# Hymba/PEER decoder layer on one core: memory tile transposed over five blocks, convolution halves by ScalarE, one row gather per block

## The chip, the cores and the metric

One core of a Trainium2 chip runs the whole layer. The metric is the device time of one launch in microseconds, as the median of several runs; the profile is of one more launch of the same program.

## The reference, cut to what matters

One decoder layer on 512 tokens of width 1024, all in float32.

```python
h = rmsnorm(x); proj = h @ w_in          # conv B | C | v | hgrn q | f | i | g, 512 columns each
y_conv = rmsnorm(B * conv3(C * v)) ; y_hgrn = hgrn2(q, f, i, g)
x = x + concat(y_conv, y_hgrn) @ w_out
kv = rmsnorm(mem) @ wkv                  # mem: 256 fixed memory tokens
x = x + cross_attention(rmsnorm(x), kv)
h = rmsnorm(x); q = h @ w_query          # 8 heads x 2 x 128
s = q . sub_keys; top-16 of each half -> 256 candidates -> top-16; gate = softmax(best)
# dense form of the expert layer: 128 blocks of 128 experts
hidden = gelu(h @ expert_down.T); y = (gate * hidden) @ expert_up; x = x + y
out = rmsnorm(x)
```

## The kernel before, in words

**Arithmetic.** Each float32 product is made of three matmuls on split operands: high by high, low by high, high by low. A weight block (128 by 1024 values, 512 KB) is loaded by SyncE into a ring of four slots; ACT copies its upper half (`high`, L539, tile `w_high`), POOL subtracts that from the whole (`low`, L432, tile `w_low`), then PE uses the block. A slot is loaded again once PE is done with it, so ACT, POOL and PE move block by block behind each other, at most four blocks apart. Each engine executes its instructions in program order.

**Front part.** Blocks 0 to 11 are column blocks of the input projection. After block 7 PE transposes the normalised memory tile: eight 128 by 128 transposes for chunks 0 to 3 (`turn_tiles`, L1335), then, inside `turn`, two transposes for each of the chunks 4 to 7 (`turn_chunk`, L1321), each of which waits until ACT (`norm_high`, L533) and DVE (`norm_gain`, L900) have taken the chunk four before it out of the same psum bank. Blocks 12 to 15 use psum banks 4 to 7, the banks of the memory tile, behind a wait for all eight chunks. Blocks 28 to 31 and 36 to 39 make the keys of the memory, 32 to 35 its values. Between block 29 and block 30 four matmuls (L1490) sum the squares of the convolution output over channels into psum bank 2; ACT turns that sum into a root (L639, L640); DVE then makes, chunk by chunk, the scaled product (L997), its upper half (L969) and its lower half (L970). The four chunks of the other group have the same two halves and come first. The output product, block 40 on, waits for all eight (`y_ready`).

**Expert part.** The last 128 blocks of the first weight are the down projection. I call them blocks 0 to 127 here; block i of the loops is high/low number 84 + i. For block i ACT makes the upper half of block i + 2, then the GELU of block i (L746), then starts a store of it (L748). The last of the four token tiles is not multiplied densely in full: for one tile (and 16 tokens of another, the "edge") the down rows of the chosen experts are gathered instead, one gather of 128 rows (512 KB) per list slot (`down_row`, L450, on POOL's queue), and DVE takes their dot products (L1069; L1066 for the edge). There are 144 gathers; the first 66 share a ring of seven buffers and stand between POOL's `low` of blocks 0 to 61. Meanwhile DVE chooses the top 16 for three token tiles, one after another (`choose`), with 22 dot products each placed at fixed points in between: numbers 0 to 21, 22 to 43, 44 to 65. Of each tile, `best_ready` comes after the 16th of its dots (number 37 for the second tile, 59 for the third), and the index and gate pieces (`hk_ready`) after the 22nd. ACT waits for `best_ready` of the second tile right before block 32's turn and of the third right before block 52's (the exponential, L778, then goes on with upper halves). PE transposes the pieces (`turn_indices`, L1645) behind block 39, before block 59 and behind block 59. After block 19 ACT starts eight small copies of the edge's row numbers (L783) in a row, and the first edge gather, number 33, waits for them.

**What sets the place of a gather.** In the loop over i, 0 to 61, POOL first executes `low` of block i and then the gathers that a formula gives it:

```python
while k < DOTS_A and i > FIRST_GATHER and (k - RING_A) * (AHEAD - 8 - FIRST_GATHER) < (i - FIRST_GATHER - 1) * (DOTS_A - RING_A):
    down_row(k)
    k += 1
```

With DOTS_A = 66, RING_A = 7 and AHEAD = 60 this is (k - 7) * 52 < (i - 1) * 59, so 59 gathers stand behind 52 blocks, some blocks with two, and the last one (65) stands behind block 53.

## Time and profile before

| what | value |
|---|---|
| median of 3 runs | 1671.52 us (1670.11 to 1676.58) |
| the profiled execution | 1673.48 us |
| its span, first to last instruction | 1671.4 us |
| PE busy | 1634.0 us, 98% |
| DVE busy | 1123.3 us, 67% |
| POOL busy | 891.1 us, 53% |
| ACT busy | 668.0 us, 40% |
| mean granted TensorE clock | 0.996 |

Times of day in the profile are microseconds from the span's start. The profiled execution was 2.0 us above the median. The front part runs to about 520, the choosing and the first 60 down blocks from 540 to 789, the rest of the first product to about 1130, and the second product to the end.

### The profile page before, as it was taken

How to read it: one execution, taken by the hardware profiler on the slowest of the kernel's cores; microseconds unless marked ns; L12 is line 12 of the kernel's file. 1: busy time of each engine (PE TensorE's matmuls, PEld its weight loads, DVE VectorE, ACT ScalarE, POOL GpSimd, SP SyncE). 2: the span in 40 equal slices, each digit the busy share in tenths (PEclk: the TensorE clock that was granted, in tenths of full speed). 3: DMA queues.
4: the chain of work that ended last, by engine and by line, in shares of the span. 5: the costliest groups of instructions: out<-in, count | busy, mean ns of one | idle time of the engine just before them, and what ended most of it. 6: DMA issues, size and time to landing. Idle time of an engine off the chain costs nothing.

```text
span 1671.4 us, 26847 instructions
## 1 busy us (share of the span) xinstructions
PE 1634.0 (98%) x9307; PEld 1452.3 (87%) x9307; DVE 1123.3 (67%) x2165; ACT 668.0 (40%) x980; POOL 891.1 (53%) x501
## 2 busy tenths in 40 slices
PE   8999999999999999999999999999999999999998
PEld 6788788767999999999999999998788878888886
DVE  4154471230283999996988887216878778888888
ACT  5352443341334343534444444433334333333334
POOL 4363374413055888996876666764444444433341
PEclk9999999999999999999999999999999999999999
DMA  5232243213634999997999999949899999999994
GB/s 189 77 101 76 76 139 104 98 39 113 218 114 170 310 330 303 306 322 226 337 337 361 355 358 345 326 166 334 293 345 334 347 317 356 347 338 337 355 341 164
DMA packets 153308, 422.11 MB, mean 253 GB/s; under 512 B 15776, under 2 KB 65952, under 8 KB 153120
## 3 DMA queue, kind: packets, MB, share of 16 engines
q1 hardware_dynamic: 90096, 234.52, 41.0%
q0 software_dynamic: 39168, 142.62, 24.4%
q10 hardware_dynamic: 23984, 44.23, 6.9%
q8 instruction: 30, 0.49, 0.1%
q14 instruction: 30, 0.25, 0.0%
HBM read 376.60 MB, written 44.17 MB: 252 GB/s over the span
## 4 chain that ended last, share of the span: by engine, by line
PE 60%; issue 20%; POOL 13%; DMA 4%; ACT 1%; DVE 1%; ACTq 0%; POOLq 0%; SPq 0%; DVEq 0%
PE psum L1349 19%; PE psum L1351 18%; PE psum L1350 18%; POOL w_low L432 11%; PE psum L1621 4%; POOL arena L450 2%; DMA arena<-up_in 2%; DMA kept<-down_in 1%; DMA arena<-hid_dram 1%; PE psum L1606 1%; ACTq L783 0%; ACT w_high L539 0%; DVE arena L1302 0%; ACT up_high L543 0%; DVE wgt_low L1266 0%
## 5 line engine op out<-in xcount | busy, mean ns | idle before, releaser
L432 POOL TENSOR_TENSOR w_low<-kept,w_high 128x1024 fp32r<-128x1024 f32 x212 | 520.3, 2456 | 405.7 <-ACT w_high L539 404.2
L1349 PE MATMUL psum<-hT_high,w_high 128*128 128x368 f32 (+2 forms) x1408 | 487.9, 347 | 9.9 <-POOL w_low L432 8.1
L1350 PE MATMUL psum<-hT_low,w_high 128*128 128x368 f32 (+2 forms) x1408 | 479.6, 341 | 0.0
L1351 PE MATMUL psum<-hT_high,w_low 128*128 128x368 f32 (+2 forms) x1408 | 479.4, 341 | 0.0
L539 ACT ACTIVATE w_high<-kept 128x1024 fp32r<-128x1024 f32 x212 | 224.1, 1058 | 212.1 <-DMA kept<-down_in 72.8
L1349 PE MATMUL psum<-up_high,wgt_high 128*128 128x512 f32 x768 | 300.1, 391 | 5.5 <-DVE wgt_low L1266 5.5
L1351 PE MATMUL psum<-up_high,wgt_low 128*128 128x512 f32 x768 | 299.4, 390 | 0.0
L1350 PE MATMUL psum<-up_low,wgt_high 128*128 128x512 f32 x768 | 299.4, 390 | 0.0
L1349 PEld LDWEIGHTS psum<-hT_high,w_high 128*128 128x128 f32 x1408 | 264.5, 188 | 25.7 <-POOL w_low L432 13.0
L1351 PEld LDWEIGHTS psum<-hT_high,w_low 128*128 128x128 f32 x1408 | 264.6, 188 | 10.3
L1350 PEld LDWEIGHTS psum<-hT_low,w_high 128*128 128x128 f32 x1408 | 264.8, 188 | 10.0 <-issue 0.5
L543 ACT ACTIVATE up_high<-arena 128x1024 fp32r<-128x1024 f32 x128 | 135.8, 1061 | 320.1 <-DMA arena<-up_in 309.5
L1237 DVE TENSOR_TENSOR up_low<-arena,up_high 128x1024 fp32r<-128x1024 f32 x128 | 156.5, 1222 | 66.1 <-ACT up_high L543 65.2
L490 POOL DMA_INDIRECT kept<-up_in,kept x64 | 101.8, 1591 | 156.2 <-DVE kept L1245 142.7
L490 POOL DMA_INDIRECT arena<-up_in,kept x64 | 108.8, 1700 | 135.4 <-DVE kept L1245 122.6
L1069 DVE CUSTOM_DVE_ANT_0 arena<-arena,psum 128x1024 f32<-128x1024 f32 x128 | 152.8, 1213 | 40.5 <-DMA arena<-down_rows,kept 40.4
L1349 PEld LDWEIGHTS psum<-up_high,wgt_high 128*128 128x128 f32 x768 | 144.5, 188 | 37.8 <-issue 8.1
L1351 PEld LDWEIGHTS psum<-up_high,wgt_low 128*128 128x128 f32 x768 | 144.6, 188 | 30.0
L1350 PEld LDWEIGHTS psum<-up_low,wgt_high 128*128 128x128 f32 x768 | 144.6, 188 | 30.0
L450 POOL DMA_INDIRECT arena<-down_rows,kept x128 | 127.9, 999 | 43.9 <-issue 16.4
L746 ACT ACTIVATE arena<-psum 128x368 f32<-128x368 f32 x112 | 53.5, 477 | 173.7 <-PE psum L1351 172.7
L1214 DVE TENSOR_TENSOR arena<-arena,psum 128x3072 bf16<-128x3072 bf16 x48 | 83.9, 1747 | 0.0
(231 smaller groups left out, 1957.9 us busy)
## 6 DMA issues: line engine op xcount, KB each, us to landing
kept<-down_in SPq DMA_DIRECT2D x128, 512.0 KB, 5.8
arena<-up_in SPq DMA_DIRECT2D x128, 512.0 KB, 5.6
kept<-front_w SPq DMA_DIRECT2D x100, 512.0 KB, 3.3
hid_dram<-arena ACTq DMA_DIRECT2D x112, 184.0 KB, 5.8
arena<-hid_dram SPq DMA_DIRECT2D x112, 184.0 KB, 6.1
gate_dram<-arena ACTq DMA_DIRECT2D x40, 512.0 KB, 7.3
under_w<-gate_dram SPq DMA_DIRECT2D x24, 640.0 KB, 7.3
arena<-gate_dram SPq DMA_DIRECT2D x8, 640.0 KB, 6.9
```

Source lines behind the costliest of these rows:

```text
L432: nc.gpsimd.tensor_tensor(w_low[:, s, :], ring[:, s, :], w_hi[:, s, :].bitcast(F32), ALU.subtract).then_inc(low_ready, 1)
L450: nc.gpsimd.indirect_dma_start(ring[slot], None, down_rows, bass.IndirectOffsetOnAxis((edge_idx if edge else idx3)[:, j:j + 1].bitcast(U32 ...
L490: nc.gpsimd.indirect_dma_start(rows_c[k % RING_C], None, up_rows, bass.IndirectOffsetOnAxis(idx3[:, k:k + 1].bitcast(U32), 0))\
L539: nc.scalar.activation(w_hi[:, s, :], ring[:, s, :], ACT.Copy).then_inc(high_ready, 1)
L543: nc.scalar.activation(up_hi[:, s, :], uraw[:, s, :], ACT.Copy).then_inc(up_high, 1)
L1069: ins = nc.vector.tensor_tensor_reduce(ring[slot], ring[slot], h_row, 1.0, 0.0, ALU.mult, ALU.add, dot3[:, j:j + 1])
L1214: nc.vector.tensor_tensor(hot_g[:, s], hot_i.rearrange("p (n q) i r -> p n q i r", q=1).to_broadcast(each), pieces[:, m:m + PAIRS].rearran ...
L1237: nc.vector.tensor_tensor(up_lo[:, s, :], uraw[:, s, :], up_hi[:, s, :].bitcast(F32), ALU.subtract).then_inc(up_low, 1)
L1349: nc.tensor.matmul(out, lhs[0], rhs[0], start=first, stop=False)
L1350: nc.tensor.matmul(out, lhs[0], rhs[1], start=False, stop=False)
L1351: return nc.tensor.matmul(out, lhs[1], rhs[0], start=False, stop=last)
L1621: ins = nc.tensor.matmul(psum[:, (2 * h + m) % 3, t % 4 * P:(t % 4 + 1) * P], hot_j[:, h % HOTS, t // 2, :, t % 2], hot_g[:, h % HOTS, t / ...
```

## The change

Five edits. The transposes of the memory tile's chunks 4 to 7 go behind blocks 8 to 11, two transposes each, and ACT's and DVE's work on these chunks follows them. ACT copies the upper halves of the four convolution chunks, in between its upper halves of the weights 34 to 37; DVE makes a product, and then the lower half of the chunk before. The sum of squares stands behind block 30. POOL's loop takes one gather per block, from block 1 on. The eight copies of the edge's row numbers stand three behind ACT's work on block 20, three behind 21 and two behind 22.

```diff
-                while k < DOTS_A and i > FIRST_GATHER and (k - RING_A) * (AHEAD - 8 - FIRST_GATHER) < (i - FIRST_GATHER - 1) * (DOTS_A - RING_A):
+                if k < DOTS_A and i > FIRST_GATHER:
                     down_row(k)
                     k += 1
...
                 if b == 7:
-                    norm_high(memn)
+                    norm_high(memn, range(0, 4))
+                if b >= 8:
+                    norm_high(memn, range(b - 4, b - 3))
...
             keys_out(29, 1)
+            keys_out(30, 2)
             act.wait_ge(conv_sum, 1)
...
-            keys_out(30, 2)
             keys_out(31, 3)
             for b in range(32, 36):
                 ahead(b)
+                act.wait_ge(conv_y, CC + b - 31)
+                nc.scalar.activation(hT_half[0][:, b - 32, :], pB[:, b - 32, :], ACT.Copy).then_inc(y_high, 1)
...
             for n in range(DT):
-                early_tiles(TURN_AT[n - 1] if n else 4 + PARTS, EXP_AT[n])
+                for i in range(TURN_AT[0] + 3, TURN_AT[0] + 4) if n == 1 else ():
+                    early_at(i)
+                early_tiles((4 + PARTS, TURN_AT[0] + 4, TURN_AT[1])[n], EXP_AT[n])
...
                     for q in range(PARTS):
+                        if q % 3 == 0:
+                            early_at(TURN_AT[n] + q // 3)
                         act.dma_start(edge_idx[q * EDGE:(q + 1) * EDGE, :],
...
-            for c in range(CC):
-                step(nc.vector.scalar_tensor_tensor(pB[:, c, :], pV[:, c, :], vec[:, V_CONV + c:V_CONV + c + 1],
-                                                    junk[:, SEQ:2 * SEQ], ALU.mult, ALU.mult))
-                y_halves(c, pB[:, c, :])
+            for c in range(CC + 1):
+                if c < CC:
+                    nc.vector.scalar_tensor_tensor(pB[:, c, :], pV[:, c, :], vec[:, V_CONV + c:V_CONV + c + 1],
+                                                   junk[:, SEQ:2 * SEQ], ALU.mult, ALU.mult).then_inc(conv_y, 1)
+                if c:
+                    dve.wait_ge(conv_y, CC + c)
+                    dve.wait_ge(y_high, c)
+                    nc.vector.tensor_tensor(hT_half[1][:, c - 1, :], pB[:, c - 1, :], hT_half[0][:, c - 1, :].bitcast(F32),
+                                            ALU.subtract).then_inc(y_ready, 1)
...
                 columns(b, b % 4, hT_half, SEQ, b % 4)
                 if b == 7:
-                    turn(memn)
+                    turn_tiles(memn)
+                if b >= 8:
+                    pe.wait_ge(memn.ready, b - 7)
+                    turn_chunk(memn, b - 4)
             pe.wait_ge(memn.ready, KC)
...
             keys(29, 1)
+            keys(30, 2)
             pe.wait_ge(conv_sq, CC)
...
-            keys(30, 2)
             keys(31, 3)
```

On POOL, the end of the loop over the blocks 0 to 61 before the change (L432 is `low` of one block, L450 a gather; the last four gathers stand behind the loop):

```order
L450 DMA arena<-down_rows,kept 128x1024 x2
L432 TENSOR_TENSOR w_low<-kept,w_high 128x1024
L450 DMA arena<-down_rows,kept 128x1024
...
L450 DMA arena<-down_rows,kept 128x1024
L432 TENSOR_TENSOR w_low<-kept,w_high 128x1024 x8
L450 DMA arena<-down_rows,kept 128x1024 x4
```

The same place with the change:

```order
L432 TENSOR_TENSOR w_low<-kept,w_high 128x1024
L450 DMA arena<-down_rows,kept 128x1024
L432 TENSOR_TENSOR w_low<-kept,w_high 128x1024
L450 DMA arena<-down_rows,kept 128x1024
L432 TENSOR_TENSOR w_low<-kept,w_high 128x1024 x2
L450 DMA arena<-down_rows,kept 128x1024 x4
```

Gather 65 stood behind `low` of block 53 and now stands behind `low` of block 59; gather 59 stood between the `low` of blocks 47 and 48 and now stands behind 53; gather 33 stood behind 24 and now stands behind 27.

On ACT, the memory tile before (L539 the upper half of a weight block, L569 an output of the input projection, L533 the upper half of a memory chunk), from block 7's output on:

```order
L569 ACTIVATE arena<-psum 128x512
L533 ACTIVATE memT_high<-psum,kept 128x256 x8
L539 ACTIVATE w_high<-kept 128x1024
L569 ACTIVATE arena<-psum 128x512
L539 ACTIVATE w_high<-kept 128x1024
```

and with the change, from the same output to the first of the four later chunks:

```order
L569 ACTIVATE arena<-psum 128x512
L533 ACTIVATE memT_high<-psum,kept 128x256 x4
L539 ACTIVATE w_high<-kept 128x1024
L569 ACTIVATE arena<-psum 128x512
L533 ACTIVATE memT_high<-psum,kept 128x256
```

Four of the eight chunks went behind the outputs of the blocks 8, 9, 10 and 11.

On ACT, from the root of the convolution's sum (its two instructions are the ones that write `kept`) before the change:

```order
L639 ACTIVATE kept<-psum,kept 128x512
L640 ACTIVATE kept<-kept 128x512
L539 ACTIVATE w_high<-kept 128x1024
L627 ACTIVATE arena<-psum 128x256
L539 ACTIVATE w_high<-kept 128x1024
L627 ACTIVATE arena<-psum 128x256
L539 ACTIVATE w_high<-kept 128x1024 x4
L632 ACTIVATE arena<-psum 128x512 x2
```

and with the change:

```order
L642 ACTIVATE kept<-psum,kept 128x512
L643 ACTIVATE kept<-kept 128x512
L539 ACTIVATE w_high<-kept 128x1024
L629 ACTIVATE arena<-psum 128x256
L539 ACTIVATE w_high<-kept 128x1024
L648 ACTIVATE hT_high<-arena 128x512
L539 ACTIVATE w_high<-kept 128x1024
L648 ACTIVATE hT_high<-arena 128x512
...
L634 ACTIVATE arena<-psum 128x512 x2
```

One key block went ahead of the root, and four copies of convolution chunks stand between the upper halves of the weights.

## Rows read from the trace of the kernel before

**Rows 1.** Who waited for whom on PE: us in total, times, longest.

```profile
PE psum L1349 <- POOL w_low L432: 8.1, 10, 2.3
PE psum L1349 <- DVE wgt_low L1266: 5.5, 5, 3.6
PE psum L1349 <- DVE hT_low L970: 2.1, 1, 2.1
```

**Rows 2.** Timeline around the memory tile: start, length, engine, line, idle before.

```profile
60.59 1.03 PE L1335 MATMUL psum<-kept,arena 128*128 128x128 f32 x8
...
63.36 1.56 PE L1321 MATMUL psum<-kept,arena 128*128 128x128 f32 x8 [1.74 <-DVE memT_low L900]
...
71.98 1.06 ACT L539 ACTIVATE w_high<-kept 128x1024 fp32r<-128x1024 f32 x1 [6.54 <-PE psum L1351]
...
77.42 1.06 ACT L539 ACTIVATE w_high<-kept 128x1024 fp32r<-128x1024 f32 x1 [3.90 <-PE psum L1351]
```

**Rows 3.** Timeline in the convolution stretch, PE and DVE.

```profile
205.97 3.70 PE L1490 MATMUL psum<-arena,kept 128*128 128x512 f32 x8 [1.17 <-ACT arena L592]
...
212.36 2.52 DVE L969 CAST hT_high<-arena 128x512 fp32r<-128x512 f32 x1
```

**Rows 4.** Timeline of the down blocks, ACT's queue and PE's gaps.

```profile
623.11 5.39 ACTq L783 DMA_DIRECT2D arena<-arena  x8
...
632.35 0.43 PE L1349 MATMUL psum<-hT_high,w_high 128*128 128x368 f32 x1 [2.29 <-POOL w_low L432]
...
674.01 0.43 PE L1349 MATMUL psum<-hT_high,w_high 128*128 128x368 f32 x1 [1.32 <-POOL w_low L432]
```

**Rows 5.** DMA issues of 560 to 760: count, median us from issue to landing.

```profile
arena<-down_rows,kept POOLq DMA_INDIRECT x39, 6.6
```

**Rows 6.** Timeline, second tile: dot 33, low of block 27, best_ready, exponential.

```profile
647.80 1.23 DVE L1066 CUSTOM_DVE_ANT_1 arena<-arena 128x1024 f32<-128x1024 f32 x1 [1.81 <-DMA arena<-down_rows,arena]
...
649.86 2.42 POOL L432 TENSOR_TENSOR w_low<-kept,w_high 128x1024 fp32r<-128x1024 f32 x1
...
669.30 0.28 DVE L1113 TENSOR_TENSOR arena<-arena 128x128 f32<-128x128 f32 x1
...
673.88 1.28 ACT L778 ACT_TABLE_LOAD   x1 [0.68 <-ACT arena L746]
```

**Rows 7.** Timeline, third tile: dots 55 and 59; low 49, 53, 54; exponential; GELU 53.

```profile
732.15 1.22 DVE L1066 CUSTOM_DVE_ANT_1 arena<-arena 128x1024 f32<-128x1024 f32 x1
...
741.76 2.43 POOL L432 TENSOR_TENSOR w_low<-kept,w_high 128x1024 fp32r<-128x1024 f32 x1
...
749.52 1.20 DVE L1069 CUSTOM_DVE_ANT_0 arena<-arena,psum 128x1024 f32<-128x1024 f32 x1
...
756.09 2.41 POOL L432 TENSOR_TENSOR w_low<-kept,w_high 128x1024 fp32r<-128x1024 f32 x1
...
758.45 1.28 ACT L778 ACT_TABLE_LOAD   x1 [0.68 <-ACT arena L746]
...
761.09 2.42 POOL L432 TENSOR_TENSOR w_low<-kept,w_high 128x1024 fp32r<-128x1024 f32 x1 [1.47 <-ACT w_high L539]
...
765.29 0.48 ACT L746 ACTIVATE arena<-psum 128x368 f32<-128x368 f32 x1 [0.64 <-PE psum L1351]
```

**Rows 8.** Timeline: dot 65, its tile's last piece, low 59, PE's transposes before block 59.

```profile
770.23 1.21 DVE L1069 CUSTOM_DVE_ANT_0 arena<-arena,psum 128x1024 f32<-128x1024 f32 x1
...
773.24 0.29 DVE L1176 TENSOR_TENSOR arena<-psum,arena 128x128 f32<-128x128 f32 x1
...
780.56 2.41 POOL L432 TENSOR_TENSOR w_low<-kept,w_high 128x1024 fp32r<-128x1024 f32 x1 [1.57 <-ACT w_high L539]
...
785.09 0.71 PE L1645 MATMUL psum<-kept,arena 128*128 128x128 f32 x5
```

**Rows 9.** Stretches behind PE's longest gap: span, busy by engine, clock, DMA share, GB/s.

```profile
1174.00:1176.00 2.00, 2.00 (x7) 1.51 (x6) 2.00 (x5) 0.77 (x3) 1.98 (x1) 0.51 0.39 134
1176.00:1178.00 2.00, 2.00 (x7) 1.63 (x6) 2.00 (x2) 1.02 (x1) 1.34 (x2) 0.64 0.29 43
```

More of the change, by code:

```diff
@@ L241, in build @@
         low_ready = sem("low_ready")
-        ld_ffn, h_row_ready, idx_ready = sem("ld_ffn"), sem("h_row_ready"), sem("idx_ready")
+        ld_ffn, idx_ready = sem("ld_ffn"), sem("idx_ready")
         ld_a = [sem(f"ld_down_rows_a{j}") for j in range(RING_A)]
@@ L289, in build @@
             sem(n) for n in ("gelu_out", "w_raw", "w_high", "w_ready", "up_done", "out_done", "x_added"))
-        ao_high, y_ready = sem("ao_high"), sem("y_ready")
+        ao_high, y_high, y_ready = sem("ao_high"), sem("y_high"), sem("y_ready")
         fin_root, fin_y, fin_pool, out_stored = (sem(n) for n in ("fin_root", "fin_y", "fin_pool", "out_stored"))
```

## The prediction

> **What bounds the kernel now.** I read the busy shares first: PE works 1634 of 1671.4 us, so the time is PE's work plus its gaps, and an edit matters only by the gaps it closes or opens. Next I read who PE waits for. The list [rows 1] holds two gaps that the edits aim at, 8.1 us behind POOL's lower halves of the weights and 2.1 us behind DVE's last convolution half, and one that they don't touch, 5.5 us in the second product. Then I went to the places themselves [rows 2 to 4]. Last I read the stretch that PE does not wait in but whose order changes: the choosing of the top 16, from 540 to 789. There DVE is busy without a pause, POOL nearly so, and the question is not who is busy but how early each gather lands before its dot product [rows 5 to 8].
>
> **Memory tile.** Block 7 ends and the first eight transposes start at 60.59. The first of the later eight starts at 63.36. ACT's next upper half, 0.2 us behind each block's end, comes at 71.98 and the one after at 77.42 [rows 2]. So block 8 with the transposes took 11.19 us where a block takes 5.44: 5.75 us to win at most. What stays: sixteen transposes, at 1.03 for eight, 2.0 us. What is new: the last chunk is transposed behind block 11, and block 12 waits for all eight chunks, since it writes their banks. Behind a block's end ACT first does an upper half and an output, then the chunk, then DVE takes it: the same chain that ran from 60.59 to 63.36 [rows 2], 2.77 us, of which two transposes cover a quarter. PE waits 2.5 us there, where it waited for nothing. ACT's and DVE's extra pieces behind the blocks 8 to 10 lie beside a 5.44 us block and cost nothing; if that cover were gone each would cost at most 0.4. Sum: 5.75 - 2.0 - 2.5 = 1.3 us won; bounds 3.7 won (no wait) and 0.4 lost (the clock falls in the new gap, at the 1.7 us worked out below).
>
> **Convolution.** PE waits 1.17 us for the last square [rows 3]; with a key block before the sum that gap goes. DVE loses four casts, 2.52 us each when POOL works beside them [rows 3], 10 us in all, so the 2.1 us wait for its last half [rows 1] goes as well. That is 3.3 us. Against it: ACT now waits for DVE's products in between the upper halves that PE needs. The fourth product is DVE's sixth instruction behind the root, and at 2.5 us each it comes 15 us behind it, while ACT also owes PE one upper half per block. Queued behind that wait are the upper halves 38 and 39, the value copies, and so POOL and PE. Nothing in the trace shows this wait. Its bounds are zero (DVE runs ahead while POOL idles) and 4.3 (the gain and a microsecond more); I take 1.6, nearer to zero since DVE speeds up as soon as POOL starves. Sum: 1.7 us won.
>
> **Edge row numbers.** The eight copies hold ACT's queue for 5.39 us, and PE's 2.29 us gap follows [rows 4]. In threes (2.0 us) they fit into a 4 us block. 2.3 us won; the first edge gather still has them in time.
>
> **One gather per block.** POOL needs 2.4 us for a lower half and about 1 for a gather, against 4 us of PE. Where the old order had two gathers in a row PE waited 1.32 us [rows 4]; that goes, 1.3 us won. But every gather from number 9 on moves back, and a block of POOL is tied to PE's progress, so POOL can't run ahead to make up for it. A gather takes 6.6 us to land [rows 5]. Three deadlines follow.
>
> *Third tile, exponential.* Gather 59 now starts behind low 53, at 756.09 + 2.41 + 0.16 = 758.7. It lands at 765.3, its dot takes 1.2, the difference behind it 0.8: `best_ready` at 767.3, but ACT wants it at 758.45 [rows 7]. 8.8 us late. Behind ACT's wait stand upper half 54, low 54 and block 54. The cover: low 54 ended at 763.5 and PE needed it at 765.0, 0.25 before GELU 53 [rows 7]: 1.5 us. Stall 7.3. It is more if DVE is late already: gather 55 now starts behind low 49, at 744.3, lands at 750.9, and its dot was at 732.15, 18.8 earlier; DVE then has 17.4 us of work without a pause to dot 59 at 749.52 [rows 7], which makes it 768.3 and the stall 10.3. POOL ran late in that stretch by its doubled gathers, so I take 9.0.
>
> *Turn before block 59.* Gather 65 starts behind low 59, 780.56 + 2.41 + 0.16 = 783.1, lands at 789.7, 19.5 us behind the old dot at 770.23. DVE's last piece ended at 773.53, so now 793.0, and PE came for it at 785.09 [rows 8]. Stall 8.0, in the frame of PE's own blocks, so it adds to the one before. Behind it stands block 59.
>
> *Second tile, exponential.* Gather 33 starts behind low 27, at 652.4; the copies' 2.3 us gone, 650.1. It lands at 656.7, 8.9 us behind the dot at 647.80. From there DVE has no pause to `best_ready` at 669.58: 678.5, while ACT comes at 673.88 - 2.3 = 671.6 [rows 6]. 6.9 us late, less 1.5 of cover as above: 5.4. If POOL, no longer doubled, is 2 us earlier: 3.4. I take 4.5.
>
> Each of these gaps is longer than the 3.64 us one, of which [rows 1] show the size, and behind which the granted clock was 0.51 and 0.64 for two stretches of 2 us, near the 1.2 GHz level: 2 * 0.49 + 2 * 0.36 = 1.7 us lost [rows 9]. Behind the 2.29 us gap [rows 4] no fall is seen. Three falls would be 5.1; I count two and a half, 4.2, since DVE gains on a slow PE.
>
> Sum here: 4.5 + 9.0 + 8.0 + 4.2 - 1.3 - 2.3 = 22.1 slower. With 1.3 and 1.7 won in front: 19.1 slower. The profiled execution of before, 1673.48, gives 1692.6; it was 2.0 above the median, so 1690.6 against the 1671.52.
>
> The landing time is the term that all three stalls share. The Trainium skill (DMA: Bandwidth & Descriptors, Anatomy of one DMA) fits such a transfer as 2.0 us plus its bytes by 436 GB/s, an estimate of 3.2 us for 512 KB; the trace's 6.6 [rows 5] is twice that, taken with other queues at work, and I go by the trace. By the page's figure each stall would be 3.4 us shorter, the sum about 9 us slower.
>
> **Rivals.**
> *The gathers land early.* The stalls leave DMA queues with less to carry, and a gather lands in half of 6.6 us. For it: nothing else loads while ACT waits. Against it: the slow ones are issued before the stall. Each stall shrinks by 3.3, the sum to 19.1 - 9.9 = 9.2: 1680.7.
> *Faster.* DVE's lead absorbs the lateness. The dots of the third tile came 12 us behind their gathers, 5 more than needed, ACT's exponential 7 us behind `best_ready` (751.45 against 758.45), the turn 11.5 behind the last piece [rows 7, 8]. If these leads hold for all three deadlines the gains stay: 1.3 + 1.7 + 2.3 + 1.3 = 6.6, which gives 1664.9. It decides at a shift of about 12 us for a gather; against it, gather 59 moves 21 us and gather 65 24.
> *No change.* One deadline alone bites, by about 8, and is paid by the gains: 1671 to 1675. It needs gather 59 or 65 to be early by 9 us; I see no row for that.
> *Worse.* ACT's wait in the convolution costs 4.3, the memory gap drops the clock, the second product's loads start late, and DVE is late at the first turn, behind block 39, too: 32 slower, 1703.5.
>
> **How the numbers follow.** Forecast 72%, early landing 8%, faster 7%, no change 5%, worse 8%. Forecast's own range: stalls of 3.4, 7.3 and 6.5, one fall, and the upper gains in front give 9 slower; 5.4, 10.3, 10, three falls and no gain in front give 29 slower. That is 1680 to 1701, which leaves out faster, no change and most of worse, 2 in 10. A change of 0.5% (8.4 us) is about what a measurement of this kernel can tell from none. Faster by more than that: 0.07, since the faster case is on the edge of it. Within: 0.08, no change with a third of the early landings. Slower: 0.85.
>
> **What would show it.** In the profile of the changed kernel PE's waits behind POOL's lower halves should rise from 8.1 to over 20, with gaps of 7 to 10 us at block 54 and of about 4 at block 34, and a new wait of about 8 us of the transposes L1645's successor for DVE before block 59. DVE should wait for gathered rows between 640 and 800, where it waited 1.8. POOL should show no pair of gathers in a row before 790. At block 12 PE should wait 2.5 us for DVE, and block 8 take 6.5 us instead of 11.2. The gaps of 1.17 and 2.1 should be gone. I am wrong if DVE's dots keep their times, or if gather 65 starts before low 56.

## The result, and the profile after

The changed kernel takes 1685.81 us as the median of four launches (1684.14 to 1688.5), the kernel before on the same chip 1670.84 (1670.11 to 1676.58). The ratio is 1.008, its 95% interval 1.0054 to 1.0105: slower by 13.4 us, between 9 and 17.5. The prediction was 1690.6, in a range of 1680 to 1701. The profiled launch of the changed kernel took 1684.14 us, its span 1682.1.

The waits of PE in the changed kernel (who waited for whom, us in total, times, longest). L1362 is the first matmul of a product, L1661 the transposes of the chosen pieces, L432 POOL's lower half of a weight block, L1189 the last piece that DVE makes of a tile:

```profile
PE psum L1362 <- POOL w_low L432: 15.7, 7, 8.5
PE psum L1661 <- DVE arena L1189: 7.7, 2, 6.3
PE psum L1362 <- DVE wgt_low L1279: 4.8, 5, 3.1
...
PE psum L1362 <- DVE memT_low L908: 2.3, 1, 2.3
...
PE psum L1362 <- ACT arena L629: 0.5, 1, 0.5
```

Against [rows 1] the waits behind POOL's lower halves have nearly doubled, though there are fewer of them, and a line that did not exist, PE behind DVE's last pieces, is the second longest. The 2.1 us for DVE's last convolution half are gone, 2.3 us for the last memory chunk are new. The places, from PE's timeline (start, length, engine, line, what, and in brackets the idle time before it with its releaser):

```profile
86.75 0.50 PE L1362 MATMUL psum<-w_high,hT_high 128*128 128x512 f32 x1 [2.29 <-DVE memT_low L908]
...
677.11 0.44 PE L1362 MATMUL psum<-hT_high,w_high 128*128 128x368 f32 x1 [3.00 <-POOL w_low L432]
...
703.15 0.77 PE L1661 MATMUL psum<-kept,arena 128*128 128x128 f32 x5 [1.41 <-DVE arena L1189]
...
768.44 0.68 PE L1362 MATMUL psum<-hT_high,w_high 128*128 128x368 f32 x1 [8.53 <-POOL w_low L432]
...
796.45 1.33 PE L1661 MATMUL psum<-kept,arena 128*128 128x128 f32 x5 [6.33 <-DVE arena L1189]
```

These are block 12, block 34 (second tile's exponential), the turn behind block 39, block 54 (third tile's exponential) and the turn before block 59. The four of the expert part sum to 19.3 us. How the 8.53 comes about is read from three engines, POOL (first two rows: gather 59 stands behind `low` of block 53), DVE (dot 59 and the difference behind it, `best_ready`) and ACT (the table for the exponential, the exponential itself):

```profile
751.95 2.42 POOL L432 TENSOR_TENSOR w_low<-kept,w_high 128x1024 fp32r<-128x1024 f32 x1
754.53 0.96 POOL L450 DMA_INDIRECT arena<-down_rows,kept  x1 [0.16 <-issue]
```

```profile
763.26 1.20 DVE L1082 CUSTOM_DVE_ANT_0 arena<-arena,psum 128x1024 f32<-128x1024 f32 x1
...
764.39 0.28 DVE L1126 TENSOR_TENSOR arena<-arena 128x128 f32<-128x128 f32 x1
```

```profile
753.11 1.28 ACT L784 ACT_TABLE_LOAD   x1 [0.68 <-ACT arena L750]
764.71 0.31 ACT L784 ACTIVATE arena<-arena 128x128 f32<-128x128 f32 x1 [10.31 <-DVE arena L1126]
```

ACT is ready at 754.39 and stands 10.31 us, with the upper half of block 54 queued behind the wait. Before the change `best_ready` was there first [rows 7]. The turn before block 59 is read in the same way: gather 65 and its dot, which waits for data, and PE's 6.33 above:

```profile
787.98 0.96 POOL L450 DMA_INDIRECT arena<-down_rows,kept  x1
```

```profile
793.09 1.22 DVE L1082 CUSTOM_DVE_ANT_0 arena<-arena,psum 128x1024 f32<-128x1024 f32 x1 [0.17 <-DMA arena<-down_rows,kept]
```

The clock fell twice. Stretches of the changed kernel (span, then busy time and count of PE, PEld, DVE, ACT, POOL, then granted clock, DMA share, GB/s):

```profile
764.00:766.00 2.00, 0.00 (x0) 0.00 (x0) 1.86 (x9) 1.28 (x3) 0.00 (x0) 0.68 0.00 0
766.00:768.00 2.00, 0.00 (x0) 0.00 (x0) 1.37 (x2) 1.74 (x2) 1.96 (x1) 0.50 0.00 0
768.00:770.00 2.00, 1.56 (x5) 1.56 (x6) 0.00 (x0) 1.42 (x2) 1.84 (x3) 0.50 0.26 94
770.00:772.00 2.00, 2.00 (x10) 2.00 (x9) 0.00 (x0) 1.06 (x1) 1.90 (x1) 0.61 0.87 162
...
798.00:800.00 2.00, 2.00 (x8) 2.00 (x7) 1.39 (x3) 1.52 (x3) 0.40 (x1) 0.50 0.00 0
800.00:802.00 2.00, 2.00 (x8) 2.00 (x8) 1.82 (x2) 0.00 (x0) 1.98 (x1) 0.50 0.00 0
```

In these rows PE runs its first 3.1 us behind the first gap near 1.2 GHz, and its first 5.8 behind the second, where the stretch from 802 to 804 still has 0.93. Behind the gap of 3.00 the granted clock is 1.00.

To see where the time went I took one mark from all traces, the start of ACT's output of the last of the down blocks; it parts the launch into a first stretch, which holds all edits, and the rest, the second product.

| profiled launch | last down output | from there to the end of the span |
|---|---|---|
| before | 1132.4 | 539.0 |
| changed | 1146.1 | 536.0 |

So the changed launch is 13.7 us behind at the mark. 1.6 us more belong to the edits: the profiled launch before lost them to a clock fall behind its memory tile that another launch with the same order did not have (shown under "Memory tile" below). The second product, which no edit touches, happened to take 3.0 less in this launch; 1.7 of that is the clock fall of [rows 9], which did not come behind this launch's wait of 3.13. Over the thirteen profiled launches of this study it took 530.9 to 540.0 (below), so it is left out of the comparison of single launches.

### The profile page after: what moved, and what is told of

It is laid out like the page before. It is cut to its first block, busy times and chain, and to the rows that moved or that the text cites. A ratio compares the mean times of both kernels' runs of the same rounds, so it can differ in the third digit from the quotient of the medians.

```text
span 1682.1 us, 26830 instructions
## 1 busy us (share of the span) xinstructions
PE 1632.9 (97%) x9307; PEld 1453.9 (86%) x9307; DVE 1114.6 (66%) x2161; ACT 670.9 (40%) x984; POOL 883.5 (53%) x501
## 4 chain that ended last, share of the span: by engine, by line
PE 60%; issue 20%; POOL 10%; DMA 4%; DVE 4%; ACT 1%; POOLq 0%; ACTq 0%; SPq 0%; DVEq 0%
PE psum L1362 19%; PE psum L1364 18%; PE psum L1363 18%; POOL w_low L432 10%; PE psum L1637 4%; DMA arena<-up_in 2%; DVE arena L1079 1%; DMA arena<-down_rows,arena 1%; DMA kept<-down_in 1%; POOL arena L450 1%; PE psum L1622 1%; DMA arena<-hid_dram 1%; DVE arena L1119 0%; DVE arena L1082 0%; ACT w_high L539 0%
## 5 line engine op out<-in xcount | busy, mean ns | idle before, releaser
L432 POOL TENSOR_TENSOR w_low<-kept,w_high 128x1024 fp32r<-128x1024 f32 x212 | 517.6, 2444 | 423.1 <-ACT w_high L539 421.9
L1362 PE MATMUL psum<-hT_high,w_high 128*128 128x368 f32 (+2 forms) x1408 | 488.4, 347 | 16.5 <-POOL w_low L432 14.8
L1362 PE MATMUL psum<-up_high,wgt_high 128*128 128x512 f32 x768 | 299.3, 390 | 4.8 <-DVE wgt_low L1279 4.8
L539 ACT ACTIVATE w_high<-kept 128x1024 fp32r<-128x1024 f32 x212 | 224.0, 1057 | 187.2 <-DMA kept<-front_w 68.4
L1362 PEld LDWEIGHTS psum<-hT_high,w_high 128*128 128x128 f32 x1408 | 265.5, 189 | 29.7 <-POOL w_low L432 17.5
L490 POOL DMA_INDIRECT arena<-up_in,kept x64 | 92.8, 1449 | 172.8 <-DVE kept L1258 161.0
L490 POOL DMA_INDIRECT kept<-up_in,kept x64 | 113.6, 1775 | 120.3 <-DVE kept L1258 109.9
L1362 PEld LDWEIGHTS psum<-up_high,wgt_high 128*128 128x128 f32 x768 | 144.1, 188 | 37.2 <-issue 7.2
L450 POOL DMA_INDIRECT arena<-down_rows,kept x128 | 127.4, 995 | 44.0 <-issue 15.2
```

What stands on the lines that cost most here:

```text
L432: nc.gpsimd.tensor_tensor(w_low[:, s, :], ring[:, s, :], w_hi[:, s, :].bitcast(F32), ALU.subtract).then_inc(low_ready, 1)
L450: nc.gpsimd.indirect_dma_start(ring[slot], None, down_rows, bass.IndirectOffsetOnAxis((edge_idx if edge else idx3)[:, j:j + 1].bitcast(U32 ...
L490: nc.gpsimd.indirect_dma_start(rows_c[k % RING_C], None, up_rows, bass.IndirectOffsetOnAxis(idx3[:, k:k + 1].bitcast(U32), 0))\
L539: nc.scalar.activation(w_hi[:, s, :], ring[:, s, :], ACT.Copy).then_inc(high_ready, 1)
L1362: nc.tensor.matmul(out, lhs[0], rhs[0], start=first, stop=False)
```

## The experiments

Each ratio is against launches of the kernel before that were measured together with it on the same chip. Gaps and marks are from one profiled launch each, and gaps of the same kernel differ from launch to launch by up to 3 us, as two kernels that ran twice show.

### One gather per block alone, and everything but that

```diff
 before, alone:
-                while k < DOTS_A and i > FIRST_GATHER and (k - RING_A) * (AHEAD - 8 - FIRST_GATHER) < ...:
+                if k < DOTS_A and i > FIRST_GATHER:
```

> The kernel before with one edit only: at most one gather behind each of POOL's lower halves, from block 1 on; memory tile, convolution and row-number copies stay as before. Theory (the loss is the later gathers meeting three deadlines): the changed kernel showed gaps of 3.0 at block 34, 8.5 at block 54, 6.3 before block 59 and 1.4 more behind block 39, 19.2 in all, and two clock falls of about 3. The 1.3 us gap of the doubled gathers goes, the 2.3 us of the copies stays, so about 20 us over the kernel before, 1691. The copies' 2.3 us hold PE up while POOL's queue of gathers goes on, so the gap at block 34 may be 2 shorter: not under 1687. Rival (the loss comes from the other four edits): within 2 us of the kernel before.

Measured: 1690.11 us, ratio 1.0121 (1.0094 to 1.0148), as expected. The mark is at 1149.2. The four gaps are there in a kernel that has no other edit:

```profile
680.95 0.67 PE L1349 MATMUL psum<-hT_high,w_high 128*128 128x368 f32 x1 [2.59 <-POOL w_low L432]
...
707.13 0.77 PE L1645 MATMUL psum<-kept,arena 128*128 128x128 f32 x5 [0.52 <-DVE arena L1176]
...
771.58 0.68 PE L1349 MATMUL psum<-hT_high,w_high 128*128 128x368 f32 x1 [7.69 <-POOL w_low L432]
...
800.53 1.33 PE L1645 MATMUL psum<-kept,arena 128*128 128x128 f32 x5 [6.58 <-DVE arena L1176]
```

```diff
 changed kernel, the gathers as before:
-                if k < DOTS_A and i > FIRST_GATHER:
+                while k < DOTS_A and i > FIRST_GATHER and (k - RING_A) * (AHEAD - 8 - FIRST_GATHER) < ...:
```

> The changed kernel with the old formula for the gathers and the other four edits kept. Theory: no stall on the three deadlines, the front part's 2.7 us and the copies' 2.3 us won, the 1.3 us gap of the doubled gathers back: 5 below the kernel before, 1666. Rival (the other edits share in the loss, or their gains are lost further on since DVE has less lead when PE is earlier): no gain, 1670 or above.

Measured: 1671.31 us, ratio 0.9988 (0.9973 to 1.0003), where 5 us, 0.997, were expected. The loss is gone, so the gathers' edit is its cause; but the gain of the other four is not there either. The mark says the same, 1133.2 against 1132.4. At block 0 this kernel is 3.8 us ahead of the one before and the 2.29 us gap of the copies [rows 4] is gone, and then, on POOL and on PE:

```profile
635.04 0.95 POOL L450 DMA_INDIRECT arena<-down_rows,kept  x1 [0.15 <-issue]
639.47 0.94 POOL L450 DMA_INDIRECT arena<-down_rows,arena  x1 [3.48 <-DMA arena<-arena]
```

```profile
642.85 0.67 PE L1362 MATMUL psum<-hT_high,w_high 128*128 128x368 f32 x1 [3.63 <-POOL w_low L432]
```

The first edge gather, number 33, stands behind block 24 in the old order and waits on POOL for the row-number copies, which now end later. Behind POOL's wait stand the lower halves, and PE waits 3.63 us; the granted clock is 0.50 for three stretches of 2 us from 642 on. In the changed kernel gather 33 stands behind block 27, at 643.73, and waits for nothing. So the split of the copies pays only together with the edit that costs the time. The next kernel has the split alone.

```diff
 before, the copies in three blocks, alone:
                     for q in range(PARTS):
+                        if q % 3 == 0:
+                            early_at(TURN_AT[n] + q // 3)
                         act.dma_start(edge_idx[q * EDGE:(q + 1) * EDGE, :],
```

> The kernel before with one edit only: the eight row-number copies in three blocks. Theory, from the kernel with the old gather formula, where POOL stood 3.5 us at gather 33 waiting for these copies and PE then stood 3.6 us with a clock fall: the copies now land later than gather 33, which stands behind block 24, wants them, so the 2.3 us gap is traded for one of 3 to 4 behind block 26 and a fall of 1.7: 1 to 4 over the kernel before. Rival (the wait for the copies came from the shifted front part, not from the split): gap gone and nothing in its place, 2.3 below the kernel before.

Measured: 1674.07 us, ratio 1.002 (0.9996 to 1.0043). The 2.29 us gap is traded for this one:

```profile
641.00 0.94 POOL L450 DMA_INDIRECT arena<-down_rows,arena  x1 [4.04 <-DVE kept L1073]
```

```profile
644.37 0.65 PE L1353 MATMUL psum<-hT_high,w_high 128*128 128x368 f32 x1 [3.83 <-POOL w_low L432]
```

The expectation held in size, its reason only in part. The last of the eight copies was issued at 634.92 and such a copy took 4.1 us from its issue in the kernel above, which puts its landing near 639.0, an estimate; the record names DVE's dot, which ended at 640.68 and freed the ring's slot. Without the 2.29 us gap POOL comes to gather 33 earlier than either is ready. Which of the two would be the last in another launch stays open.

### The third exponential two blocks later

```diff
 changed kernel:
                 early_tiles((4 + PARTS, TURN_AT[0] + 4, TURN_AT[1])[n], EXP_AT[n])
+                for i in range(EXP_AT[-1], EXP_AT[-1] + 2) if n == DT - 1 else ():
+                    early_at(i)
                 act.wait_ge(best_ready, n + 2)
...
-            for i in range(EXP_AT[-1], AHEAD - 1):
+            for i in range(EXP_AT[-1] + 2, AHEAD - 1):
```

> The changed kernel with ACT's wait for the third tile's best list, and the exponential behind it, two blocks later (behind the work of block 53 instead of 51); no gather moves. Theory (program order: ACT asks too early): the 8.5 us gap of PE at block 54 shrinks to under 1, one clock fall goes; the turn before block 59 is set by gather 65, whose place is tied to blocks that now run 8 us earlier, so its wait stays near 6. In all 9 us below the changed kernel, about 1676. Rival (DVE is simply late by then, the wait moves to the turn before block 59): the gap at 54 goes, the one before 59 grows by as much, the time stays at 1685.

Measured: 1682.64 us, ratio 1.0068 (1.0052 to 1.0085): 2 us below the changed kernel by the ratios, 3 by the medians, where 9 were expected. In the profiled launch the mark is at 1140.0, 6.0 ahead of the changed kernel's, and the four gaps sum to 13.0 in place of 19.3; the second product took 3.0 more and gave half of that back. The gap at block 54 went from 8.53 to 0.52, as expected; the one before block 59 did not stay:

```profile
790.79 1.33 PE L1663 MATMUL psum<-kept,arena 128*128 128x128 f32 x5 [9.43 <-DVE arena L1191]
```

The theory had the turn's wait tied to blocks, since gather 65 is. Gather 65 did come 7.7 us earlier, at 780.24, but its dot only 5.7, at 787.44. PE came for the pieces 8.8 us earlier. Gather 64 shows why: it was issued at 776.70, and its dot waited for the data until 784.09, 7.4 us; in the changed kernel the same gather took 5.5 and gather 65 5.1. The DMA share while they were under way doesn't tell these apart, 0.80 to 1.04 here and 0.85 to 0.95 there, so what made the landing longer stays open. Each theory gave half of it: the wait is one of program order, and a stall that is removed is partly paid for by the next deadline.

### The gathers one and two blocks earlier

```diff
 changed kernel, one pair:
-                if k < DOTS_A and i > FIRST_GATHER:
+                while k < DOTS_A and i > FIRST_GATHER and k <= i + RING_A - 1 + (i >= 12):
 two pairs:
+                while k < DOTS_A and i > FIRST_GATHER and k <= i + RING_A - 1 + (i >= 12) + (i >= 20):
```

> The changed kernel with one gather per block but for block 12, which gets a pair: every later gather one block, 4 us, earlier. Theory (a stall is lateness less cover, four for four): gap at block 54 from 8.5 to about 4.5, before block 59 from 6.3 to about 2.3, at block 34 from 3.0 to 0, no clock fall or one; 1684.1 less 11 less 2 to 4, about 1670. Rival (DVE has no slack of its own, its dots wait for data all along): the two long gaps shrink by 2 at most, 1677 or above.

> The changed kernel with one gather per block but for two blocks, 12 and 20, which get a pair: every gather from the second pair on starts two blocks, 8 us, earlier. Theory (each stall is its gather's lateness less a fixed cover): gap at block 34 gone, at block 54 from 8.5 to about 0.5, before block 59 from 6.3 to 0, no clock fall; so all 19 us of stalls and 3 of clock go but for a microsecond: 1664, some 6 below the kernel before. Rival (landing time, not the place, makes the lateness; a pair costs PE 1.3 us each time): gaps shrink by less than half, 1675 or above.

Measured with one pair, in a single launch: 1676.85 us, the mark at 1139.1. With two pairs: 1664.43 us, ratio 0.9956 (0.9938 to 0.9974), the mark at 1131.6 in a launch that was the slowest of ten. The time with one pair is near the rival's 1677 and not the 1670 that was expected: this launch had a clock fall at 87, one at 763, one at 790 and one at 1180. The gaps, read below, are nearer the theory's. With one pair there is no gap at block 34, and the two long ones are

```profile
764.82 0.68 PE L1362 MATMUL psum<-hT_high,w_high 128*128 128x368 f32 x1 [5.45 <-POOL w_low L432]
...
790.59 1.33 PE L1661 MATMUL psum<-kept,arena 128*128 128x128 f32 x5 [3.20 <-DVE arena L1189]
```

| gathers earlier by | gap at block 54 | gap before block 59 |
|---|---|---|
| 0 blocks | 8.53 | 6.33 |
| 1 block, 4 us | 5.45 | 3.20 |
| 2 blocks, 8 us | 2.03 | none |

Each block takes 3.1 to 3.4 us off a gap in these single launches, not quite the 4 that the theory gave, and more than the 2 of the rival. Nothing changed here but the place of the gathers, so their lateness is the cause, and it goes nearly one for one.

The two pairs make gather 33 stand behind block 25, and there it waited 3.34 us for the copies again:

```profile
642.61 0.96 POOL L450 DMA_INDIRECT arena<-down_rows,arena  x1 [3.34 <-DMA arena<-arena]
```

The same kernel once more, measured together with other launches:

> The kernel with pairs at the blocks 12 and 20 once more, on the chip of the others of this call. Theory (its gain of 0.4% was its order's): ratio 0.995 to 0.998 again, first product's end near 1131.6 of the profile. Rival (the gain was of that chip's second product, whose 3.5 us wait for DVE is there in some launches and not in others): ratio 0.998 to 1.001.

Measured: 1665.39 us, ratio 0.9951 (0.993 to 0.9972), the mark at 1126.9. The gain is the order's. In this launch there was no gap behind the copies, and 0.66 at block 54 in place of 2.03, so the second block takes 4.8 off that gap here and 3.4 above: one launch's small gaps are not a kernel's.

### All extra pairs behind the copies

```diff
 changed kernel:
-                if k < DOTS_A and i > FIRST_GATHER:
+                while k < DOTS_A and i > FIRST_GATHER and k <= i + RING_A - 1 + (i >= 28) + (i >= 32) + (i >= 37) + (i >= 42):
```

> The changed kernel with one gather per block up to block 27, so that gather 33 keeps its place behind the row-number copies, and pairs at blocks 28, 32, 37 and 42: gather 43 two, gathers 59 and 65 four blocks earlier than in the changed kernel. Theory: no wait for the copies on POOL (3.3 us where two pairs stood at blocks 12 and 20), no gap behind block 39, at block 54 or before block 59, no clock fall; the 3.0 us gap at block 34 stays, since it follows dot 33 with no pause in DVE. 1684 less 16.2 less 3.4 of clock: about 1664.5 of the profiled execution, 1663 to 1665 as median. Rival (each pair costs PE 1.3, as in the kernel before): 5 more, 1669.

> The kernel with pairs at the blocks 28, 32, 37 and 42 once more. Its profiled launch took 1661.9, nine others 1667 to 1675. Theory (that launch lacked the wait of PE for DVE's first halves in the second product, 3.1 to 4.1 us long in the nine other profiles, and the clock fall behind it, and nothing else): a second profile ends the first product near 1129 again and takes 537 to 540 from there, 1668. Rival (the first product varies as well): its end lies 3 or more from 1129.

Measured: 1670.66 us, ratio 1.000 (0.9978 to 1.0023), and the second time 1671.02, ratio 0.9985 (0.9972 to 0.9999). So 1663 to 1665 was wrong, and the rival of 1669 closer. The first profiled launch, 1661.9, had all that was expected of it; its gap at block 34 was 2.19. It was the fastest of ten. The second shows what the others are like:

```profile
681.55 0.68 PE L1362 MATMUL psum<-hT_high,w_high 128*128 128x368 f32 x1 [5.18 <-POOL w_low L432]
...
1174.29 0.77 PE L1362 MATMUL psum<-up_high,wgt_high 128*128 128x512 f32 x1 [4.00 <-DVE wgt_low L1279]
```

Its mark is at 1133.6, 4.7 behind the first launch's, and the rest took 539.3 against 530.9. Of the 4.7, 1.6 were lost right behind block 12, where the clock fell behind the same 2.29 us gap behind which it had stayed up in the first launch. Both parts vary: the rival of the second expectation holds for the first product, and the theory's 4 us wait of the second product is there too. With gather 33 behind block 27 the second tile has no lead at all. Its best list came 1.9 us later against ACT than in the first launch: gather 33 took 6.0 us from its issue to its dot in place of 5.6, and the chain from that dot to the list 23.7 in place of 22.3. Both go into the gap at block 34.

```diff
 the kernel above, and:
-                    norm_high(memn, range(b - 4, b - 3))
+                    norm_high(memn, ((4,), (5,), (6, 7), ())[b - 8])
...
-                act.wait_ge(conv_y, CC + b - 31)
-                nc.scalar.activation(hT_half[0][:, b - 32, :], ...
+                for c in ((0,), (1,), (), (2,))[b - 32]:
+                    act.wait_ge(conv_y, CC + c + 1)
+                    nc.scalar.activation(hT_half[0][:, c, :], ...
             values_out(0, 2)
+            act.wait_ge(conv_y, 2 * CC)
+            nc.scalar.activation(hT_half[0][:, 3, :], ...
...
+                if n == 1:
+                    early_at(EXP_AT[n])
                 act.wait_ge(best_ready, n + 2)
...
-                    pe.wait_ge(memn.ready, b - 7)
-                    turn_chunk(memn, b - 4)
+                    for c in ((4,), (5,), (6, 7), ())[b - 8]:
+                        pe.wait_ge(memn.ready, c - 3)
+                        turn_chunk(memn, c)
```

> late_pairs with three further moves: memory chunk 7 transposed behind block 10 with chunk 6, so none behind 11; ACT's upper halves of the convolution chunks 2 and 3 one upper half of the weights later; the second tile's exponential one block later. Theory: the 2.3 us gap at block 12, the 0.9 and 0.5 in the convolution and the 3.0 at block 34 go: 6.5 below late_pairs, about 1657. Rival for the last move: the wait goes to the transposes behind block 39, as it went to those before block 59 when the third exponential was moved, and 3 us of it are kept: 1660.

Measured: 1669.64 us, ratio 0.9987 (0.9968 to 1.0006), 1 below the kernel above where 6.5 or 3.5 were expected. Of its three moves the memory chunk did what it should, no gap at block 12. ACT's later copies did not: the gap in the convolution was 1.45 instead of 0.92. The later second exponential cleared block 34, and a wait came up at the turn behind block 39, as its rival said:

```profile
702.10 0.77 PE L1669 MATMUL psum<-kept,arena 128*128 128x128 f32 x5 [1.55 <-DVE arena L1196]
```

Six small gaps of 0.5 to 1.2 between 650 and 762 sum to 5.1. That they took the rest is not shown, since two launches of the kernel above differ by 4.7 at the mark.

### One pair early, two late, and the memory chunk

```diff
 changed kernel:
-                if k < DOTS_A and i > FIRST_GATHER:
+                while k < DOTS_A and i > FIRST_GATHER and k <= i + RING_A - 1 + (i >= 12) + (i >= 37) + (i >= 44):
...
-                    norm_high(memn, range(b - 4, b - 3))
+                    norm_high(memn, ((4,), (5,), (6, 7), ())[b - 8])
...
-                    pe.wait_ge(memn.ready, b - 7)
-                    turn_chunk(memn, b - 4)
+                    for c in ((4,), (5,), (6, 7), ())[b - 8]:
+                        pe.wait_ge(memn.ready, c - 3)
+                        turn_chunk(memn, c)
```

> The changed kernel with one gather per block but for pairs at the blocks 12, 37 and 44, and memory chunk 7 transposed behind block 10 with chunk 6. Theory: with one early pair gather 33 stands behind block 26, where the row-number copies have landed, and the second tile is in time (one early pair alone: no gap at block 34, none at the copies); gather 59 stands behind block 50, 65 behind 56, two blocks earlier than with one pair, where the gaps were 5.4 and 3.2: both go, with their clock falls. The 2.3 at block 12 goes, as it did before. GELU 127 at about 1124 of the profile, against 1132 of the kernel before: 8 below it, ratio 0.995. Rival (each pair costs PE 1.3 and more by the DMA load): 1128, ratio 0.9975.

Measured: 1665.0 us, ratio 0.9952 (0.9935 to 0.997), the mark at 1122.9. This is faster than both kernels, by 0.5% and by some 1.3%. The kernel with two early pairs, in which only the gathers have moved, has the same ratio, 0.9956 and 0.9951; what the memory chunk and the late pairs add is seen in the gaps and the mark, not in the times. PE's waits:

```profile
PE psum L1362 <- POOL w_low L432: 5.2, 8, 0.9
PE psum L1362 <- DVE wgt_low L1279: 4.8, 3, 3.1
```

```profile
663.81 1.28 ACT L784 ACT_TABLE_LOAD   x1 [0.67 <-ACT arena L750]
665.43 0.31 ACT L784 ACTIVATE arena<-arena 128x128 f32<-128x128 f32 x1 [0.33 <-DVE arena L1126]
...
750.51 0.31 ACT L784 ACTIVATE arena<-arena 128x128 f32<-128x128 f32 x1 [0.85 <-issue]
```

15.7 us of waits behind lower halves have become 5.2, the longest 0.9; the transposes of the pieces do not wait; block 12 starts at 84.27 in place of 86.75, with no gap. ACT's two exponentials wait 0.33 and 0.85 us behind their table loads. The second wait is also one for the list, though the row names no releaser: DVE's last instruction for it ran from 750.18 to 750.47. The mark lies 9.5 us ahead of the kernel before, 1.6 of them for the clock fall of that launch; the ratio shows 8.0.

## Why the prediction was right

The sign, the places and the mechanism were as worked out: gathers that come later meet three fixed points in program order. The experiments show that the loss is the gathers' alone. The sizes came out close in part by luck: the gain of the memory tile was a clock fall of the launch before, and in two of the three stalls errors cancelled. PE's waits behind POOL's lower halves rose to 15.7, not to over 20 as the prediction had as a sign. By its steps:

**Memory tile.** Forecast 1.3 won, with a new wait of 2.5 at block 12. Block 12 starts at 86.75 with the change and started at 88.10 before: 1.35 won; the wait is 2.29. That the gain fits is luck. In the profiled launch before, the clock fell right behind the later transposes:

```profile
64.00:66.00 2.00, 2.00 (x8) 1.48 (x8) 1.98 (x5) 1.44 (x4) 0.28 (x1) 0.68 0.00 0
66.00:68.00 2.00, 2.00 (x6) 1.61 (x5) 0.00 (x0) 0.00 (x0) 0.00 (x0) 0.50 0.00 0
```

That is 3.4 us near 1.2 GHz, or 1.7 us lost, and these 1.7 are in the 5.75 that the prediction put down as "to win at most". The kernel with one gather per block alone has the old order here, and in its launch the clock stayed up: block 12 started at 86.47, 0.3 us before the changed kernel's. So without that fall the edit of the memory tile won nothing. The new wait can bring a fall too. In the changed kernel's launch the clock stayed at 1.00 behind it, as forecast; among the eight launches of kernels with this wait it fell in three. What does win is chunk 7 behind block 10, which takes the wait away (84.27 in the last kernel).

**Convolution.** Forecast 1.7 won. At PE's next wait that both launches have, 1.33 us for DVE, the changed kernel is 3.06 us ahead (296.78 against 299.84), so 1.7 came from here. At block 0 it is 2.73 ahead: a wait near 457 was 0.94 in this launch and 0.60 in the one before, and between nothing and 2.10 in the others. The gaps of 1.17 and 2.1 are gone, and ACT's wait costs PE 0.94 and 0.47 where 1.6 was put. ACT waited 3.75 us for the third product:

```profile
212.43 5.71 DVE L1006 SCALAR_TENSOR_TENSOR arena<-arena,kept 128x512 f32<-128x512 f32 x2
218.07 2.90 DVE L1011 TENSOR_TENSOR hT_low<-arena,hT_high 128x512 fp32r<-128x512 f32 x1
220.89 2.88 DVE L1006 SCALAR_TENSOR_TENSOR arena<-arena,kept 128x512 f32<-128x512 f32 x1
223.69 0.68 DVE L1011 TENSOR_TENSOR hT_low<-arena,hT_high 128x512 fp32r<-128x512 f32 x1
```

The turn that the prediction named, DVE speeding up as soon as POOL starves, is the step from 2.90 to 0.68 for the same instruction: POOL had nothing to do from 223.2 to 225.5. The Trainium skill (SBUF — State Buffer, SBUF: two separate sides) says that a DVE instruction with two SBUF inputs and a GpSimd instruction that reads SBUF exclude each other on a shared pair of ports, each for its whole length; these rows agree.

**Edge row numbers.** Forecast 2.3 won. Between the outputs of blocks 19 and 26 the changed kernel wins 2.6, so it held, and "the first edge gather still has them in time" held as well. What the step did not say is that this holds only by the gather edit; with the old order both kernels of the first experiments lose it again and more.

**Pairs.** Forecast 1.3 won. The gap is gone, and a second one of 0.8 at 737 too: beside the four, PE's gaps between the outputs of the blocks 31 and 60 sum to 0.1 us, before to 2.5. Ahead of block 19 another 1.2 are won, as in the kernel with that edit alone. That is 3.6, so the term was under-sized by 2.3.

**The three stalls.** Forecast 4.5, 9.0 and 8.0; measured 3.00, 8.53 and 6.33. The term that they share, the landing of a gather, was put at the 6.6 us of [rows 5] and was mis-sized: from issue to dot gather 33 took 5.1 us (643.73 to 648.86), gather 55 5.4 and gather 65 5.1, each with a dot that waited for the data. For the turn before block 59 that is the whole miss but 0.2.

For the two exponentials it is not, since DVE's work behind the landing took longer by about as much: 23.0 us from dot 33 to the best list where 21.8 were put, and 19.3 from dot 55 to dot 59 where 17.4 were, with no pause in either. The two dots themselves had grown, from 1.23 [rows 6] to 3.88 and from 1.22 [rows 7] to 3.44, each beside a lower half of POOL's:

```profile
648.86 3.88 DVE L1079 CUSTOM_DVE_ANT_1 arena<-arena 128x1024 f32<-128x1024 f32 x1 [1.78 <-DMA arena<-down_rows,arena]
...
743.96 3.44 DVE L1079 CUSTOM_DVE_ANT_1 arena<-arena 128x1024 f32<-128x1024 f32 x1 [0.91 <-DMA arena<-down_rows,arena]
```

```profile
649.23 2.41 POOL L432 TENSOR_TENSOR w_low<-kept,w_high 128x1024 fp32r<-128x1024 f32 x1
...
743.90 2.41 POOL L432 TENSOR_TENSOR w_low<-kept,w_high 128x1024 fp32r<-128x1024 f32 x1
```

Both dots end 1.1 us behind that lower half. The prediction took the time of DVE's chain as fixed. The second tile's gap still came out under the forecast because POOL was 2 us earlier, the case that the prediction priced at 3.4: ACT came for the list 23.6 us behind the issue of gather 33. In the third tile the list was 11.6 us behind ACT's coming, as the second of its two estimates had it (11.8), so the lateness was DVE's. But the gap was 8.5 and not that estimate's 10.3: the cover was 3.1 and not 1.5, of which 1.28 is ACT's table load, done before it waits. The 9.0 between the two estimates fits the 8.53 by luck.

The other price that the prediction had, the 3.2 us of the Trainium skill (DMA: Bandwidth & Descriptors, Anatomy of one DMA), is further off: the shortest landing before a waiting dot in this stretch was 4.2, of gather 61, issued 3.6 us behind the end of the long stall, and gather 60 just ahead of it took 4.7. The median of the gathers from 560 to 760 that are not the edge's fell too, from [rows 5] to

```profile
arena<-down_rows,kept POOLq DMA_INDIRECT x32, 5.6
```

so the rival of an early landing was right in direction, and came with 1.5 us where it had 3.3. Its reason, queues left empty by a stall, fits the gathers 60 and 61 alone, and gather 63, three blocks on, still took 4.8; gather 33 stands behind no stall, and at gather 65 the DMA share was back at 0.85 to 0.95.

**The first turn.** 1.4 us behind block 39, named only under "worse" and not priced.

**Clock.** Forecast two and a half falls of 1.7, 4.2 us. Two came, but longer ones. From the output of block 31 to that of block 60 the changed kernel lost 20.7 us. PE's gaps there sum to 19.4 where they were 2.5, which leaves 3.8 for the clock. The part of a fall that lies inside a gap costs nothing, the part behind it half of its length: the 3.1 and 5.8 us of the rows above make 4.5, so the two ways agree to 0.7.

**The sum.** Forecast 22.1 slower from block 0 on and 3.0 faster ahead of it. Measured to the mark: 16.4 slower and 2.7 faster, 13.7 in all, against 19.1. Of the 5.7 by which the part from block 0 on was over-estimated 2.2 are the stalls (with the unpriced turn counted), 2.3 the small pair gaps, 0.4 the clock, 0.3 the copies, and 0.4 are won behind block 60. Against a launch before without the fall at its memory tile the part ahead would be 1.1 faster and the whole 15.3 slower. The difference of the medians is 15.0, the ratio's 13.4.

## What to carry to other kernels

An engine that issues transfers in between its work on blocks has a budget of one issue per block, but its consumers have deadlines; count from each deadline back (landing, work of the consumer, lead) before the issues are spread evenly, and put the extra issue where the producer's own inputs are there and the deadline is still ahead. A stall that is repaired by moving the wait is paid in part at the next deadline if the data are late (8.0 us taken off one gap here, 3.1 added to the next), while each extra issue early takes from all of them. An edit whose gain hangs on the place of another, like the split copies here, has to be tried with and without that other. Before a stretch is called time to win, look whether the clock fell in it, and whether it does so in a second launch: here 1.7 of 5.75 us were such a fall.

## What the runs showed of the hardware that was not expected

**Gap length did not sort the clock falls.** The same gap of PE in the same place brought a fall in one launch and none in the next. Behind the 1.74 us at the old memory tile the clock fell in two of three launches. Behind the 2.29 us at block 12 it fell in three of eight (in the kernels with the later exponential and with one pair, and in the second launch with four late pairs, from 87 to 90.5), and in the changed kernel it did not. The gap of 3.00 us in the changed kernel left the granted clock at 1.00 too. In the kernel with two pairs the gap at 763 was shorter and the clock fell:

```profile
762.00:764.00 2.00, 0.99 (x6) 0.99 (x7) 2.00 (x3) 1.51 (x3) 1.85 (x2) 1.00 0.87 291
764.00:766.00 2.00, 2.00 (x10) 2.00 (x9) 2.00 (x4) 1.29 (x2) 1.99 (x2) 0.61 0.75 170
766.00:768.00 2.00, 2.00 (x8) 2.00 (x8) 1.94 (x2) 0.00 (x0) 1.82 (x3) 0.53 0.68 260
```

PE had stood for 2.03 us. In the kernel with one gather per block alone it fell to 0.50 behind gaps of 2.02 and 2.59, in the one with the later exponential behind 2.55, and in the one with two pairs not behind 2.42. In the second product it fell behind a gap of 3.08 in the fastest kernel and not behind one of 3.13 in the changed one. All gaps of 3.2 us and more in these thirteen launches, that at the very start apart, had a fall. Below that it can't be told from the gap.

**The second product takes 530.9 to 540.0 us for the same instructions.** In twelve of thirteen launches PE waits 3.1 to 4.2 us for DVE's first halves there, in eleven with a clock fall; in the fastest launch, the first of the kernel with four late pairs, its longest wait there is 0.6. No run here tells what decides it.

**A dot product of DVE took up to three times its length beside POOL.** In the launches before and after, 23 of the edge's dot products began within a lower half of POOL's or up to 0.6 us ahead of one. All of them ended 1.1 us behind that lower half and took 1.3 to 4.1 us. The nine that met none, or began 0.9 us ahead of one, took 1.2. So when a gather's place moves, the work behind it can change its length.
